# A gathered expert layer: eight tokens' rows in transfers of their own at four steps, two stages of the plan moved

## The reference

```python
def layer_c(h, w_in, v_norm, w_spatial, b_spatial, w_out):
    ...
    mixed = jnp.einsum('gts,bnsgc->bntgc', w, v) + b_spatial.T[:, :, None]
    return (u * mixed.reshape(b_, s_, SGU_WIDTH)) @ w_out

def peer(h, w_q, subkeys, u_tab, v_tab):
    ...
        u_sel = u_tab[ii]
        act = jax.nn.gelu(jnp.einsum('td,tkd->tk', xi, u_sel).astype(jnp.float32), approximate=False)
        w = (gi * act).astype(v_tab.dtype)
        return jnp.einsum('tk,tkd->td', w, v_tab[ii])
```

## Time and profile before

| what | value |
|---|---|
| runs shown | 1612.63, 1613.42, 1613.43 us, median 1613.42 |
| profiled execution, its own time | 1613.09 us |
| its span, first to last instruction | 1611.4 us |
| PE busy | 1434.2 us (89%) |
| DVE busy | 980.2 us (61%) |
| ACT busy | 668.2 us (41%) |
| POOL busy | 654.7 us (41%) |
| bytes moved, rate over the span | 626.57 MB, 389 GB/s |
| of it the gathered rows (queue q0) | 536.90 MB |

### The profile page before, as it was taken

How to read it: one execution, slowest core, us unless ns; L and a number is a source line. 1 busy time by engine, 2 the same in 40 slices (tenths; PEclk the granted TensorE clock), 3 DMA queues, 4 the chain that set the end, 5 groups by cost and what they waited for, 6 DMA issues and landing times.

```text
span 1611.4 us, 14849 instructions
## 1 busy us (share of the span) xinstructions
PE 1434.2 (89%) x4450; PEld 706.0 (44%) x4450; DVE 980.2 (61%) x2487; ACT 668.2 (41%) x1841; POOL 654.7 (41%) x535
## 2 busy tenths in 40 slices
PE   7999989999957998998988999999899889797776
PEld 6546455465412433443343545445335345342222
DVE  1226578758748756753347756566556778777744
ACT  1514544534525334442244534343334454444433
POOL 1001344444434333353345333333344544556673
PEclk9999999999989999999999999999999999999999
DMA  5443999999999999999999999999999999999996
GB/s 212 158 155 129 422 421 422 421 421 421 421 422 421 393 423 421 421 422 421 422 419 407 422 421 421 421 422 373 423 421 409 422 420 401 421 421 421 421 421 280
DMA packets 86656, 626.57 MB, mean 389 GB/s; under 512 B 9760, under 2 KB 9904, under 8 KB 10672
## 3 DMA queue, kind: packets, MB, share of 16 engines
q0 software_dynamic: 73728, 536.90, 80.6%
q1 hardware_dynamic: 12672, 88.45, 13.5%
q10 hardware_dynamic: 176, 0.28, 0.1%
HBM read 624.54 MB, written 1.05 MB: 388 GB/s over the span
## 4 chain that ended last, share of the span: by engine, by line
PE 42%; DMA 33%; DVE 10%; ACT 6%; issue 4%; POOL 3%; SPq 0%; POOLq 0%; DVEq 0%; ACTq 0%
DMA ring<-in_peer_uv,experts 33%; PE acc L1580 22%; DVE ring L1229 6%; PE work L1367 5%; PE work L1350 5%; POOL ring L686 3%; PE work L1339 3%; PE work L1382 2%; PE acc L1543 1%; ACT diag L878 1%; ACT gelus L876 1%; ACT L875 1%; PE work L1434 1%; ACT gelus L875 1%; ACT L869 1%
## 5 line engine op out<-in xcount | busy, mean ns | idle before, releaser
L1580 PE MATMUL acc<-ring,diag 128*128 128x512 f32 x2048 | 979.0, 612 | 158.7 <-ACT diag L878 156.6
L686 POOL DMA_INDIRECT ring<-in_peer_uv,experts x512 | 645.3, 1260 | 845.1 <-PE acc L1580 700.3
L1229 DVE CUSTOM_DVE_ANT_0 ring<-ring,h 128x1024 f32<-128x1024 f32 x512 | 624.9, 1226 | 440.4 <-DMA ring<-in_peer_uv,experts 427.8
L1580 PEld LDWEIGHTS acc<-ring,diag 128*128 128x128 f32 x2048 | 367.7, 191 | 687.5 <-ACT diag L878 349.5
L875 ACT ACTIVATE gelus<-dots 128x1 f32<-128x1 f32 x512 | 103.2, 201 | 694.5 <-DVE dots L1229 693.9
L878 ACT ACTIVATE diag<-ident,gelus 128x128 f32<-128x128 f32 x512 | 205.5, 401 | 16.7
L876 ACT ACTIVATE gelus<-gelus,gates 128x1 f32<-128x1 f32 x512 | 150.8, 295 | 16.6
L1350 PE MATMUL work<-weights,hT 128*128 128x512 f32 x192 | 88.1, 592 | 0.0
L1367 PEld LDWEIGHTS work<-hT,weights 128*128 128x128 f32 x576 | 69.8, 192 | 16.3 <-issue 16.3
L1367 PE MATMUL work<-hT,weights 128*128 128x128 f32 x576 | 70.1, 275 | 0.0
L1350 PEld LDWEIGHTS work<-weights,hT 128*128 128x128 f32 x192 | 36.2, 191 | 43.1 <-issue 43.0
(11 more groups left out here) (211 smaller groups left out, 898.3 us busy)
## 6 DMA issues: line engine op xcount, KB each, us to landing
weights<-in_c_w_in SPq DMA_DIRECT2D x14, 1024.0 KB, 9.1
more<-in_c_w_in SPq DMA_DIRECT2D x11, 1024.0 KB
weights<-in_ab_w_in SPq DMA_DIRECT2D x10, 1024.0 KB, 5.2
weights<-in_peer_w_q SPq DMA_DIRECT2D x10, 1024.0 KB, 9.2
ring<-in_peer_uv,experts POOLq DMA_INDIRECT x512
weights<-in_ab_w_out SPq DMA_DIRECT2D x4, 1024.0 KB, 5.2
weights<-in_c_w_out SPq DMA_DIRECT2D x4, 1024.0 KB, 12.2
scores<-in_c_w_out SPq DMA_DIRECT2D x4, 1024.0 KB
```

The costliest lines, as they stand in the source:

```text
L686: pool.indirect_dma_start(ring[:, t % SLOTS, :], None, uv_rows, bass.IndirectOffsetOnAxis(ap=experts[:, b, step:step + 1], axis=0))\
L1229: nc.vector.tensor_tensor_reduce(out=ring[:, k, 0:D], in0=ring[:, k, 0:D], in1=h[:, b, :], scale=1.0, scalar=0.0, op0=ALU.mult, op1=ALU.ad ...
L1580: last = nc.tensor.matmul(acc[2 * b + n][:, :], diag[:, k, :], ring[:, k, D + n * CH:D + (n + 1) * CH], start=False, stop=True, skip_group ...
```

## The change

Three things are changed.

1. In the trunk of block 1 the spatial groups 2, 3 and 0 start 4 steps apart instead of 2 (phase (1,0), steps 62 to 73).
2. The final norm of block 0 and its store stand at steps 100 to 102 of phase (1,1) instead of 14 to 16.
3. For head 6 of phase (1,1), steps 96, 100, 104 and 108 (every fourth rank) get an extra step. A mask `inside` is 1 on partitions 12 to 15 and 44 to 47. In the step's own transfer the ids of those eight tokens are raised by 65536, past the table, and `bounds_check` leaves rows with such ids out. The extra step's transfer goes to partitions 0 to 52 only (53 rows), with the ids of all other tokens raised, so that it brings the eight rows. The gates are split in the same way, so each row counts once. An extra step takes a ring slot, and a dot product, three ScalarE operations and TensorE's products over all 128 partitions like any other.

With it come the masks, made on GpSimd behind step 4 of phase (1,1) (stage GROUPS: two memsets, four affine selects, each waiting for the one before), five small VectorE operations more for the ids and two more for the gates. From the plan, the room table changes in six of 42 pieces of weights: `scores1` takes the place of other rooms in some, with as many loads as before.

```diff
+EVERY = 4
+EXTRA_HEADS = ((1, 1, 6),)
+EXTRAS = [(layer, b, hd * TOPK + k) for layer, b, hd in EXTRA_HEADS for k in range(0, TOPK, EVERY)]
+GROUP = 3
+REACH = 53
+FAR = 2.0 ** 16
+
+def first_row(phase):
+    return phase * STEPS + sum(2 * layer + b < phase for layer, b, _ in EXTRAS)
+
+def rows_of(layer, b, i0, i1):
+    t = first_row(2 * layer + b) + i0 + sum((layer, b) == (l, c) and at < i0 for l, c, at in EXTRAS)
+    for step in range(i0, i1):
+        yield t, step, None
+        t += 1
+        if (layer, b, step) in EXTRAS:
+            yield t, step, EXTRAS.index((layer, b, step))
+            t += 1
...
-                    out += mixed(int(at) + 2 + 2 * i, b, k)
+                    out += mixed(int(at) + 2 + 4 * i, b, k)
...
-        + gather_with(1, 1, [(1, ("ADD", 1, 0))], parts_for(1), normed(14, "final", 0) + [(16, ("STORE", 0))])
+        + gather_with(1, 1, [(1, ("ADD", 1, 0)), (4, ("GROUPS",))], parts_for(1), normed(100, "final", 0) + [(102, ("STORE", 0))])
...
+                    for tile, first in ((inside, 4 * GROUP), (lower, 4 * GROUP + 32)):
+                        linked(pool.memset(tile, 1.0))
+                        linked(pool.affine_select(out=tile, in_=tile, compare_op=ALU.is_ge, fill=0.0, base=-first,
+                                                  pattern=[[0, TOPK]], channel_multiplier=1))
+                        linked(pool.affine_select(out=tile, in_=tile, compare_op=ALU.is_ge, fill=0.0, base=first + 3,
+                                                  pattern=[[0, TOPK]], channel_multiplier=-1))
...
+                        if extra is not None:
+                            pool.indirect_dma_start(
+                                ring[0:REACH, t % SLOTS, :], None, uv_rows,
+                                bass.IndirectOffsetOnAxis(ap=moved[0:REACH, extra:extra + 1], axis=0),
+                                bounds_check=2 * NK * NK - 1, oob_is_err=False).then_inc(row_in[t % SLOTS], 16)
+                        elif (layer, b, step) in EXTRAS:
+                            pool.indirect_dma_start(
+                                ring[:, t % SLOTS, :], None, uv_rows,
+                                bass.IndirectOffsetOnAxis(ap=experts[:, b, step:step + 1], axis=0),
+                                bounds_check=2 * NK * NK - 1, oob_is_err=False).then_inc(row_in[t % SLOTS], 16)
...
+                    link(nc.vector.tensor_tensor(picked[:, 0, :], picked[:, 0, :], picked[:, 1, :], ALU.add))
+                    link(nc.vector.tensor_tensor(inside[:, own], inside[:, own], lower[:, own], ALU.add))
+                    link(nc.vector.tensor_scalar(outside[:, own], inside[:, own], -1.0, 1.0, ALU.mult, ALU.add))
+                    link(nc.vector.tensor_copy(head_of(experts, b, hd), picked[:, 0, :]))
+                    nc.vector.scalar_tensor_tensor(moved[:, own], outside[:, own], FAR, few, ALU.mult, ALU.add)
+                    nc.vector.scalar_tensor_tensor(head_of(experts, b, hd)[:, ::EVERY], inside[:, own], FAR, few,
+                                                   ALU.mult, ALU.add).then_inc(experts_ready, 1)
...
+                    link(nc.vector.tensor_tensor(moved_gates[:, own], g[:, ::EVERY], inside[:, own], ALU.mult))
+                    link(nc.vector.tensor_tensor(g[:, ::EVERY], g[:, ::EVERY], outside[:, own], ALU.mult))
```

More of the change, by code:

```diff
@@ L385, in trunk @@
         stick_masks = sb("stick_masks", [P, 4, P])
+        inside, outside, lower = (stick_masks[:, 0, i * TOPK:(i + 1) * TOPK] for i in range(3))
+        moved = stick_masks[:, 1, 0:len(EXTRAS)].bitcast(i32)
+        moved_gates = stick_masks[:, 2, 0:len(EXTRAS)]
         last_decay = sb("last_decay", [P, 2])
@@ L670, in _ @@
                     layer, b, i0, i1 = args
-                    for step in range(i0, i1):
-                        t = first_step(layer, b) + step
+                    for t, step, extra in rows_of(layer, b, i0, i1):
                         pool.wait_ge(experts_ready, 1 + IDS_ORDER[layer, b, step // TOPK])
@@ L871, in _ @@
                     layer, b, i0, i1 = args
-                    for step in range(i0, i1):
-                        k = (first_step(layer, b) + step) % SLOTS
-                        act.wait_ge(dots_done, first_step(layer, b) + step + 1)
+                    for t, step, extra in rows_of(layer, b, i0, i1):
+                        k = t % SLOTS
+                        act.wait_ge(dots_done, t + 1)
+                        gate = gates[:, b, step:step + 1] if extra is None else moved_gates[:, extra:extra + 1]
                         link(nc.scalar.activation(gelus[:, k:k + 1], dots[:, k:k + 1], ACT.Gelu))
                         link(nc.scalar.activation(gelus[:, k:k + 1], gelus[:, k:k + 1], ACT.Copy,
-                                                  scale=gates[:, b, step:step + 1]))
+                                                  scale=gate))
                         nc.scalar.activation(diag[:, k, :], ident[:, :], ACT.Copy, scale=gelus[:, k:k + 1])\
@@ L1121, in expert_ids @@
                                              ALU.mult, ALU.add))
+                if (layer, b, hd) in EXTRA_HEADS:
+                    j = EXTRAS.index((layer, b, hd * TOPK))
+                    own = slice(j, j + TOPK // EVERY)
+                    few = picked[:, 0, ::EVERY]
+                    dve.wait_ge(groups_made, 6)
+                    link(nc.vector.tensor_tensor(picked[:, 0, :], picked[:, 0, :], picked[:, 1, :], ALU.add))
[5 more added lines that the diff above has]
+                                                   ALU.mult, ALU.add).then_inc(experts_ready, 1)
+                    return
                 nc.vector.tensor_tensor(head_of(experts, b, hd), picked[:, 0, :], picked[:, 1, :], ALU.add)\
@@ L1575, in _ @@
                     layer, b, i0, i1 = args
-                    for step in range(i0, i1):
-                        pe.wait_ge(diag_ready, first_step(layer, b) + step + 1)
-                        k = (first_step(layer, b) + step) % SLOTS
+                    for t, step, extra in rows_of(layer, b, i0, i1):
+                        pe.wait_ge(diag_ready, t + 1)
+                        k = t % SLOTS
                         for n in range(2):
@@ L1582, in _ @@
                                                     start=False, stop=True, skip_group_check=True)
-                            if n == 0 and first_step(layer, b) + step + 1 == first_step(2, 0):
+                            if n == 0 and t + 1 == first_row(4):
                                 last.then_inc(first_half_full, 1)
```

24 lines of the change are left out of this document (15 added, 9 removed).

## The result

The changed kernel takes 1618.44 us (median of 6 runs, 1617.41 to 1620.11) against 1612.09 us of the kernel before on the same chip (6 runs, 1609.85 to 1613.43): ratio 1.0043, 95% interval 1.0033 to 1.0053. It is slower, by 0.43%, and outside the range of 1608.8 to 1615.8. The profiled execution took 1618.27 us with a span of 1616.5.

A forecast was written before the change was run, and what follows sets the result against it. One late DMA engine was taken to bound the kernel; relieved, the others end at 1599.5, less 2.0, plus 2.5 for the norm: 1600.0 against 1601.7, so 1613.42 - 1.7 = 1611.7 us, range 1608.8 to 1615.8.

The forecast's parts named there:

- What bounds the kernel: Gathered-row transfers: one late DMA engine's work sets the time, to 1601.7 us, plus a tail of 9.7 us.
- The rival in which another engine is the late one: The eight rows are not the late engine's, so nothing is gained: 1614.7 us, at most 1617.4; chance 0.25.
- The relief: Four steps without the eight rows take 9.96 us off the late engine, done near 1591.8 us.
- The extra's rows: Each extra's eight rows fall on one engine, another each time, which ends 2.49 us later; worst of four 1599.5 us.
- Left-out rows at nothing: Rows left out of transfers by the bound check cost nothing.
- The extra steps on the compute engines, masks, ids: Extra compute, masks behind step 4 and id operations near step 78 are covered by the transfers and cost nothing.
- GpSimd's bound-checked issues: Rival: eight bound-checked issues get longer, deciding from 1.3 us each; 1617.4 us at 2 us each; chance 0.08.
- The spatial groups' spacing: Wider spacing behind steps 62 to 73 gives nothing, 4.6 us at most; as a rival 1609.4 us, chance 0.05.
- The norm: Moving the final norm gains 2.0 us at step 16 and costs 2.5 us at steps 101 and 102.
- The range around the forecast: The forecast's own range, 1610.0 to 1614.0 us around 1611.7, with the terms 2.49 and 2.5 at their bounds.

The follow-up runs named there:

- experiment 7: experiment 4 without extra steps: in four steps the eight rows are left out and nobody brings them, result incomplete; 1608.9 us, 0.9977 of the kernel before.
- experiment 1: The changed kernel with the final norm of block 0 and its store back at steps 14 to 16; 1616.42 us, 1.0035 of the kernel before.
- experiment 4: The changed kernel with only its extra steps kept: norm back at 14 to 16, group spacing back at 2; 1616.41 us, 1.0036 of the kernel before.
- experiment 8: experiment 4 with each extra's eight rows brought by two transfers of four rows, none left out in the extra; 1616.61 us, 1.0035 of the kernel before.
- experiment 11: experiment 4 with one extra transfer, the first, instead of four; 1612.09 us, 1.0001 of the kernel before.
- experiment 2: The changed kernel without extra transfers or bound checks, norm at step 100 and spacing 4 kept; 1611.86 us, 1.0001 of the kernel before.
- experiment 3: The changed kernel with other eight tokens, partitions 8 to 11 and 40 to 43; 1620.1 us, 1.0050 of the kernel before.
- experiment 5: experiment 4 with no row moved: own transfers bring all 128 rows, extras leave out all 53; 1615.04 us, 1.0021 of the kernel before.
- experiment 9: experiment 4 with extra steps that issue no transfer, gates of zero, own transfers whole; 1611.82 us, 0.9998 of the kernel before.
- experiment 10: experiment 4 with extra transfers of 128 partitions, 120 left out, so the eight rows come by their usual engine; 1612.28 us, 1.0004 of the kernel before.
- experiment 13: experiment 4 with one extra of 128 partitions, 120 left out, its eight tokens moved by 64 partitions; 1610.14 us, 0.9992 of the kernel before.
- experiment 14: experiment 13 with two extras, at steps 96 and 104, moved by 64 and by 68 partitions; 1611.27 us, 0.9998 of the kernel before.
- experiment 12: experiment 11 with the extra writing to partitions 64 to 116, the eight tokens' rows of that step missing; 1611.18 us, 0.9996 of the kernel before.
- experiment 6: experiment 4 with extras of 16 live rows at gate zero, no bound checks, nothing left out; 1621.05 us, 1.0062 of the kernel before.

## Why the prediction was wrong

**What bounds the kernel: right.** One late DMA engine sets the end, and its partitions were the ones taken; experiment 7 shows both. The rival in which another engine is the late one falls.

**The relief: right in kind, too large in effect, and then undone.** I took 9.96 us off the late engine, so that the other fifteen set the end, from 1601.7 to 1597.5 before the norm's term, 4.2 us. The bare relief of experiment 7 gave 1612.15 - 1608.9 = 3.2 us, 1612.15 being the kernel before in its series.

**The extra's rows: the step that failed.** The prediction says: "I take all eight on one engine, another one each time: the engines hit end 2.49 us later". It weighed which engine brings the rows, and never where they are written. The two steps ahead of the relieved one show that the partitions count. They take 7.2 to 7.8 us in all five traces read in which another engine writes to partitions 12 to 15 and 44 to 47 (the changed kernel and experiments 1, 4, 8 and 11). They take 4.95 to 4.99 us where no other engine does (before and experiments 2, 3, 5, 7, 9, 10, 13 and 14), and 5.4 us in experiment 12.

The late engine writes without pause to these partitions, and the extra makes a second engine write to them. Both then crawl: packets of 8192 B take 0.31 us elsewhere, and the packet records of the one extra have 14 of 0.57 us or more between 1517.7 and 1522.5. Eight of them follow each other end to start, 4.8 us in all, and the other six fall in the same stretch. The records name no engine; that the eight are the extra's and the six are of the late one is inferred. As an estimate, the late engine loses 8 x 0.3 = 2.4 us; VectorE shows 2.6. That is just what the relief gives it (2.49 us less some 0.1 for the left-out rows), and the extra's engine needs 4.8 us for work that I priced at 2.49. So this way gives no relief. With partitions 64 to 116 packets of 0.6 us are there again, but the late engine is left nearly undisturbed.

The Trainium skill has the rule that I passed over, on other pages than the one I cited: "SBUF — State Buffer", section "Door 1: The DMA port swizzle", puts partitions 12 to 15 and 44 to 47 on one of 16 DMA ports, and "Advanced Engine Details and Errata", section "DMA Bandwidth Details", gives each port 27.2 GB/s. By that rule one engine at 26.3 GB/s fills its port, and rows moved to another engine still queue at the same one. The traces agree: 0.31 us a packet alone and twice that for two engines. Experiment 6 fits too, if each of the sixteen engines writes one of its rows: they would meet at four such groups. The rate falls to 366 to 389 GB/s there, and the two steps take 6.5 us.

**Left-out rows at nothing: right in full transfers, open in the extras.** The page counts 90112 packets after and 86656 before, all 3456 more of them under 512 B. Experiment 7 leaves out 32 rows of full transfers and has as many packets as before, 32 more of them small: one small packet in place of each row. An extra of 53 partitions brings 864 packets, 53 x 16 + 16, whether eight of its rows are live (experiment 11) or none (experiment 5); one of 128 partitions brings 144, 128 + 16 (experiment 10). In a full transfer eight left-out rows cost an engine about 0.1 us. Whether the many small packets of an extra of 53 partitions are as harmless is less sure: experiment 5 is slower by 0.21%, where experiment 9, without these transfers, isn't, and its trace, of the fastest run, doesn't show why. Up to 2.9 us of the loss can be of this kind. **This stays open.**

**Four extras cost more than four times one.** One is even, four lose 5.0 us (experiment 4). The shared partitions account for a relief that is given back and for some 2.4 us too much on the extra's engine each time, 0.3 us in the mean of 16 engines. That isn't enough for a mean engine that loses 5.2 us in experiment 4. Experiment 9 shows 2.8 us of such a loss without any extra transfer, hidden by the late engine's lag. The engines lead each other by what the eight slots allow; in the changed kernel the issues of 1520 to 1531 wait for TensorE and so for the last engine, the share falls to 0.86 and the front engines run dry. That a chain of slowed steps uses up the lead in this way is argued from these stages; how the 5.0 us are made up stays open.

**The extra steps on the compute engines, masks, ids: right for the end** (experiment 9), though not for the other engines' lead, which shrinks by the 2.8 us above. **GpSimd's bound-checked issues: that rival falls.** In the changed kernel they take 1.0 to 1.9 us as the others do, one of them 2.6 us, and experiment 10 has all eight at 1.0004. **The spatial groups' spacing: right at nothing** (4 against 1, and 2).

**The norm: near.** I gave 2.0 us back at step 16 and took 2.5 at step 102. The stall and the dip came as described: share 0.66, GpSimd's wait 9.35 us, and 6.2 us for the mean engine, within the 2.0 to 7.0 that I had. Beside extras it is worth about 2 us (changed kernel against experiment 1, not resolved); without them nothing.

The sum in place of mine, for the start of the last dot: late engine at 1601.7; relief some 9.6 us off (four times 2.49 less 0.1), and up to 4 x 2.4 = 9.6 on for the shared partitions, so it stays near where it was. The changed kernel's last dot starts at 1606.9, 5.2 us later, and that of the extras alone at 1604.8, 3 us later. These last terms are read off and not derived; lead lost by the others is the account that fits.

**The range around the forecast.** It was given as 1610.0 to 1614.0, "the terms 2.49 and 2.5 at their bounds". At those bounds the terms give 1607.0 (0.31 and nothing) to 1612.1 us (2.49 and 2.9), so this range doesn't follow from the sum. The measured time lies above both.

## What to carry to other kernels

Before rows are moved to another engine, look at the partitions that they land in: a write to partitions that a busy engine already fills slowed both here. If rows are to be moved, move them to other partitions too, and only as much as the next engine is ahead; the gain of that, 1.5 us in experiment 13, is likely and not shown. A DMA share of 1.0 with a falling rate says that packets take longer, and not why: transfers that meet do it, but experiment 9 has 390 GB/s at 0.99 with no second transfer. And a loss can hide under the lag of the last engine, so look at the rate and not only at the time.

## What the runs showed of the hardware

- Two engines that write to the same eight partitions (12 to 15, 44 to 47) slow each other, packets of 8192 B from 0.31 to about 0.6 us: two steps take 7.55 us in place of 4.98, and 5.36 when the same transfer writes elsewhere (experiments 11 and 12).
- A transfer of 128 partitions with 120 of them left out runs beside a full stream, four times, at no cost to the time that can be measured (1.0004, 0.9995 to 1.0013), while one of 16 rows, all live, also four times, costs 0.62%.
- A row left out of a transfer of 128 partitions is one packet of under 512 B; eight of them take about 0.1 us of an engine, where eight live rows take 2.49. A transfer of 53 partitions brings 864 packets, live rows or not.
